# The second and the last unit of each feed-forward stage take the joined matmul form of the others

## The reference, cut to what matters

```
def _swiglu(h, w_gate, w_up, w_down):
    return (jax.nn.silu(h @ w_gate) * (h @ w_up)) @ w_down
x = x + 0.5 * _swiglu(_rmsnorm(x, g[0]), ffn_w_gate[layer, 0], ffn_w_up[layer, 0], ffn_w_down[layer, 0])
```

## Time and profile before

| What | Value |
|---|---|
| median of 3 runs | 1509.05 us (1508.98 to 1510.08) |
| the profiled execution's own time | 1512.8 us |
| its span | 1511.0 us |
| TensorE busy | 1488.1 us, 98% |
| TensorE weight loads | 1300.1 us, 86% |
| VectorE / ScalarE / GpSimd busy | 1128.9 / 835.3 / 474.2 us |
| joined up steps (line 648, 16 matmuls each) | 1808 matmuls, so 113 units |

### The profile page before, as it was taken

The page is one execution under the profiler, slowest core; times in us unless marked ns, Lnnn a source line. Parts: engine busy times, 40 slices in busy tenths (PEclk is TensorE's granted clock), DMA queues, the critical chain, the costliest instruction groups (busy, mean ns, idle before and its releaser), DMA issues. The chain is left out here.

```text
span 1511.0 us, 26410 instructions
## 1 busy us (share of the span) xinstructions
PE 1488.1 (98%) x9944; PEld 1300.1 (86%) x9944; DVE 1128.9 (75%) x1286; ACT 835.3 (55%) x1288; POOL 474.2 (31%) x209
## 2 busy tenths in 40 slices
PE   8999999999999999999999999999999999999998
PEld 7888889898888888888987888888888887888887
DVE  6877856567777777787765687877777789878785
ACT  6555465336545555545576645456455578654544
POOL 2443400000434327343352343433343300144342
PEclk9999999999999999999999999999999999999999
DMA  7655542134655546555442555555555553265552
GB/s 269 232 182 193 180 140 72 59 114 152 223 194 182 193 135 225 193 194 185 166 169 85 195 186 195 191 178 185 194 182 192 181 181 126 98 212 190 188 197 75
DMA packets 48815, 260.04 MB, mean 172 GB/s; under 512 B 5584, under 2 KB 5968, under 8 KB 28144
## 3 DMA queue, kind: packets, MB, share of 16 engines
q1 hardware_dynamic: 29520, 190.49, 36.1%
q10 hardware_dynamic: 19152, 68.53, 14.1%
q0 software_dynamic: 80, 0.14, 0.0%
HBM read 258.08 MB, written 1.05 MB: 171 GB/s over the span
## 5 line engine op out<-in xcount | busy, mean ns | idle before, releaser
L378 POOL TENSOR_TENSOR dn_lo<-raw_dn,dn_hi 128x1024 fp32r<-128x1024 f32 x138 | 435.8, 3158 | 791.1 <-ACT dn_hi L361 783.8
L365 DVE TENSOR_TENSOR gu_lo<-raw_gu,gu_hi 128x2048 fp32r<-128x2048 f32 x161 | 370.2, 2299 | 163.6 <-ACT gu_hi L351 162.0
L648 PE MATMUL banks<-h_both,gu_hi 128*128 128x512 f32 x1808 | 428.2, 389 | 0.0
L648 PEld LDWEIGHTS banks<-h_both,gu_hi 128*128 128x128 f32 x1808 | 339.3, 188 | 70.5
L559 DVE TENSOR_TENSOR act_lo<-act,act_hi 128x256 fp32r<-128x256 f32 x132 | 312.0, 2364 | 9.0 <-ACT act_hi L525 9.0
L351 ACT CAST gu_hi<-raw_gu 128x2048 fp32r<-128x2048 f32 x160 | 303.9, 1900 | 12.0 <-PE banks L385 12.0
L517 ACT COPY arena<-banks 128x256 f32<-128x256 f32 x113 | 42.1, 372 | 373.3 <-PE banks L656 373.3
L656 PEld LDWEIGHTS banks<-h_both,gu_lo 128*128 128x128 f32 x1808 | 231.8, 191 | 8.8
L656 PE MATMUL banks<-h_both,gu_lo 128*128 128x256 f32 x1808 | 234.5, 283 | 0.0
L385 PE MATMUL banks<-dn_hi,act_hi 128*128 128x512 f32 x528 | 207.9, 394 | 1.8 <-DVE act_lo L559 1.4
L385 PE MATMUL banks<-dn_lo,act_hi 128*128 128x512 f32 x528 | 207.1, 392 | 0.0
(11 more groups left out here) (390 smaller groups left out, 1648.6 us busy)
## 6 DMA issues: line engine op xcount, KB each, us to landing
raw_gu<-units_gu SPq DMA_DIRECT2D x161, 1024.0 KB, 4.8
raw_dn<-units_dn ACTq DMA_DIRECT2D x130, 512.0 KB, 3.5
raw_dn<-units_dn SPq DMA_DIRECT2D x32, 512.0 KB, 3.5
x<-x_in SPq DMA_DIRECT2D x2, 512.0 KB, 5.1
cst<-constants SPq DMA_DIRECT2D x1, 688.0 KB, 5.8
raw_gu<-units_gu SPq DMA_DIRECT2D x2, 256.0 KB, 6.2
raw_gu<-units_gu SPq DMA_DIRECT2D x1, 512.0 KB, 7.4
lora<-low_rank SPq DMA_DIRECT2D x1, 512.0 KB, 6.7
```

What stands on the lines that cost most here:

```text
L365: nc.vector.tensor_tensor(gu_lo[:, p, :], raw_gu[:, p, :], gu_hi[:, p, :].bitcast(F32), ALU.subtract).then_inc(gu_lo_ready, 1)
L378: nc.gpsimd.tensor_tensor(dn_lo[:, p, 0:n], raw_dn[:, p, 0:n], dn_hi[:, p, 0:n].bitcast(F32), ALU.subtract).then_inc(dn_lo_ready, 1)
L648: ins = nc.tensor.matmul(banks[:, 2 * p + side, :], gu_hi[:, p, w], h_both[:, k, :, :].rearrange("p i t -> p (i t)"), start=first and k == ...
```

## The change

FIRST_BOTH goes from 2 to 1 and LAST_BOTH from 20 to 21. Unit 1 and unit 21 of each of the six stages take the joined form, and so does unit 20 of the final stage: 6 + 6 + 1 = 13 units. Unit 0 stays separate. The special code of unit 1 goes (`high_first`, `second_up_high_first`, the branch `both` of `ffn_up`); in the first stage TensorE waits for the gate half of `gu_hi` before the gate matmuls and for the whole before the up matmuls (`gate_only`). The weights for a unit two ahead are split only where there is one (`if ahead`).

```diff
-        FIRST_BOTH, LAST_BOTH = 2, FFN_UNITS - 2
+        FIRST_BOTH, LAST_BOTH = 1, FFN_UNITS - 1
...
-            if both is not None:
+            if ahead and both is not None:
                 hi_gu(act, pair + 1, p)
...
-                lo_gu(dve, pair + 1, p)
+                if ahead:
+                    lo_gu(dve, pair + 1, p)
...
-        def ffn_up(pe, pair, p, f, both=True):
-            if both:
-                ffn_up_joined(pe, pair, p, f)
-                return
-            pe.wait_ge(gu_lo_ready, 2 * pair + p + 1)
-            count(pe, act_ready, f - 1)
-            for side in range(2):
-                for k in range(KD):
-                    w = slice((side * KD + k) * P, (side * KD + k + 1) * P)
-                    ins = three_products(banks[:, 2 * p, side * T:(side + 1) * T],
...
-        def ffn_up_joined(pe, pair, p, f):
-            pe.wait_ge(gu_hi_ready, 2 * pair + p + 1)
+        def ffn_up(pe, pair, p, f, gate_only=False):
+            if not gate_only:
+                pe.wait_ge(gu_hi_ready, 2 * pair + p + 1)
             count(pe, act_ready, f - 1)
             high_weights(p, 0)
+            if gate_only:
+                pe.wait_ge(gu_hi_ready, 2 * pair + p + 1)
             high_weights(p, 1)
...
-            ffn_act(act, b, 1, f + 1, True)
+            ffn_act(act, b, 1, f + 1, True, n + 1)
...
-            ffn_act(act, b + i, 1, f + 2 * i + 1, False, load=s + 1 < len(stages))
+            ffn_act(act, b + i, 1, f + 2 * i + 1, False, n + 2 * i + 1, load=s + 1 < len(stages))
...
-            ffn_dve(dve, b, 1, f + 1, True, None, SECOND_BANK, FIRST_UP_BANKS[1] if high_first(s) else None)
+            ffn_dve(dve, b, 1, f + 1, True, n + 1)
...
-            ffn_dve(dve, b + i, 1, f + 2 * i + 1, False)
+            ffn_dve(dve, b + i, 1, f + 2 * i + 1, False, n + 2 * i + 1)
...
-            if high_first(s):
-                second_up_high_first(pe, s)
-            else:
-                ffn_up(pe, b, 1, f + 1, both=False)
+            if s == 0:
+                pe.wait_ge(second_gate, 1)
+            ffn_up(pe, b, 1, f + 1, gate_only=s == 0)
```

More of the change, by code:

```diff
@@ L527, in ffn_act @@
                 hi_gu(act, pair + 1, p)
-        FIRST_UP_BANKS = (5, 3)
-        SECOND_BANK = 2
+        FIRST_UP_BANK = 5
         def seam_bank(s):
@@ L568, in ffn_first_up @@
                 pe.wait_ge(gu_lo_ready, 2 * pair + 1)
-            gate, up = banks[:, bank, 0:T], banks[:, FIRST_UP_BANKS[0] if s == 0 else bank, T:2 * T]
+            gate, up = banks[:, bank, 0:T], banks[:, FIRST_UP_BANK if s == 0 else bank, T:2 * T]
             def gate_part(part, b):
@@ L605, in ffn_first_up, with high_weights @@
             ins.then_inc(gu_used, 1)
[L607 to L612, removed]
-            for side in range(2):
-                if s == 0:
-                    pe.wait_ge((second_gate, gu_hi_ready)[side], side + 1)
-                else:
-                    pe.wait_ge(gu_hi_ready, 2 * pair + 2)
-                for k in range(KD):
-                    w = slice((side * KD + k) * P, (side * KD + k + 1) * P)
[L620 to L629, removed]
-        def ffn_up(pe, pair, p, f, both=True):
-            if both:
-                ffn_up_joined(pe, pair, p, f)
-                return
-            pe.wait_ge(gu_lo_ready, 2 * pair + p + 1)
-            count(pe, act_ready, f - 1)
-            for side in range(2):
-                for k in range(KD):
-                    w = slice((side * KD + k) * P, (side * KD + k + 1) * P)
-                    ins = three_products(banks[:, 2 * p, side * T:(side + 1) * T],
[L641 to L645, removed]
+        def high_weights(p, side):
             for k in range(KD):
@@ L648, in high_weights, with low_weights @@
                 ins = nc.tensor.matmul(banks[:, 2 * p + side, :], gu_hi[:, p, w],
-                                       h_both[:, k, :, :].rearrange("p i t -> p (i t)"), start=first and k == 0,
-                                       stop=not first and k == KD - 1, skip_group_check=not first)
+                                       h_both[:, k, :, :].rearrange("p i t -> p (i t)"), start=k == 0, stop=False)
             return ins
-        def low_weights(p, side, first=False):
+        def low_weights(p, side):
             for k in range(KD):
                 w = slice((side * KD + k) * P, (side * KD + k + 1) * P)
-                ins = nc.tensor.matmul(banks[:, 2 * p + side, 0:T], gu_lo[:, p, w], h_hi[:, k, :], start=first and k == 0,
-                                       stop=not first and k == KD - 1, skip_group_check=first)
-            return ins
-        def ffn_up_joined(pe, pair, p, f):
-            pe.wait_ge(gu_hi_ready, 2 * pair + p + 1)
+                ins = nc.tensor.matmul(banks[:, 2 * p + side, 0:T], gu_lo[:, p, w], h_hi[:, k, :], start=False,
+                                       stop=k == KD - 1)
+            return ins
+        def ffn_up(pe, pair, p, f, gate_only=False):
+            if not gate_only:
+                pe.wait_ge(gu_hi_ready, 2 * pair + p + 1)
             count(pe, act_ready, f - 1)
             high_weights(p, 0)
+            if gate_only:
+                pe.wait_ge(gu_hi_ready, 2 * pair + p + 1)
             high_weights(p, 1)
@@ L776, in ffn_all_act @@
             i = HALF - 1
-            ffn_act(act, b + i, 0, f + 2 * i, s + 1 < len(stages), n + 2 * i if s + 1 < len(stages) else None)
-            ffn_act(act, b + i, 1, f + 2 * i + 1, False, load=s + 1 < len(stages))
+            ffn_act(act, b + i, 0, f + 2 * i, s + 1 < len(stages), n + 2 * i)
+            ffn_act(act, b + i, 1, f + 2 * i + 1, False, n + 2 * i + 1, load=s + 1 < len(stages))
         def ffn_all_dve(dve, s):
@@ L804, in ffn_all_dve @@
             n = both_before(f)
-            ffn_dve(dve, b, 0, f, True, None, seam_bank(s), FIRST_UP_BANKS[0] if s == 0 else None)
-            ffn_dve(dve, b, 1, f + 1, True, None, SECOND_BANK, FIRST_UP_BANKS[1] if high_first(s) else None)
+            ffn_dve(dve, b, 0, f, True, None, seam_bank(s), FIRST_UP_BANK if s == 0 else None)
+            ffn_dve(dve, b, 1, f + 1, True, n + 1)
             with dve.Fori(1, HALF - 1) as i:
@@ L810, in ffn_all_dve @@
             i = HALF - 1
-            ffn_dve(dve, b + i, 0, f + 2 * i, s + 1 < len(stages), n + 2 * i if s + 1 < len(stages) else None)
-            ffn_dve(dve, b + i, 1, f + 2 * i + 1, False)
+            ffn_dve(dve, b + i, 0, f + 2 * i, s + 1 < len(stages), n + 2 * i)
+            ffn_dve(dve, b + i, 1, f + 2 * i + 1, False, n + 2 * i + 1)
             add_to_x(dve, s)
@@ L846, in ffn_all_pe @@
             i = HALF - 2
-            ffn_up(pe, b + 1 + i, 0, f + 2 + 2 * i, both=s + 1 < len(stages))
+            ffn_up(pe, b + 1 + i, 0, f + 2 + 2 * i)
             ffn_down(pe, b + i, 1, f + 1 + 2 * i, False, False)
-            ffn_up(pe, b + 1 + i, 1, f + 3 + 2 * i, both=False)
+            ffn_up(pe, b + 1 + i, 1, f + 3 + 2 * i)
             ffn_down(pe, b + 1 + i, 0, f + 2 + 2 * i, False, False)
```

## The result

The changed kernel takes 1529.24 us (median of 4 runs, 1526.37 to 1533.64) against 1509.09 us before (1508.98 to 1510.08): a ratio of 1.0132, 95% interval 1.0119 to 1.0145. It is slower by 20 us; 1527 were forecast. Its profiled execution took 1530.55 us.

What follows compares the result with a forecast made beforehand. TensorE, busy 98% of the span, was taken as the bound. Waits at unit 1 of 15.45 us less 1.54 saved gave +13.9, 1523.0 us from the 1509.05 median; 4.2 for clock falls made 1527 us, range 1520 to 1534.

Steps and rivals of the forecast that it cites:

- The saving of 0.22 us a joined unit: TensorE's up step: 5.54 us joined against 5.76 separate, so 2.86 us over 13 units if nothing else moves.
- The formula of the Trainium skill: Up step: N/2.4 + 2.5 ns a matmul, so 16 fewer save only 0.04 us a unit; the prediction followed the trace instead.
- Units 21 and 20 hidden: Last units: act_lo 2.45 us behind the up step, 0.29 us ahead of down(21), so the full 1.54 us is saved.
- Unit 1, the chain of 9.63 to 9.66 us from the L365 ahead: At down(1): act_lo ends that late, so TensorE waits 3.9 us in stage one, 2.9 in two, 3.7 in five.
- The fifth stage: Unit 1 there: late dn_hi and POOL's dn_lo add 0.79 us; wait 3.7 us at down(1), stage cost 3.17 us.
- The 6.85 us: Second stage, unit 1: time from the end of L365 to down(1); a shorter chain would cause no wait.
- Nothing at down(2): Unit 2, no longer the first joined unit: no TensorE wait, down(2) coming 8.29 us behind down(1).
- The sum without the clock: Whole kernel: 15.45 us of stage shifts at unit 1 less 1.54 saved at the last units, +13.9 us.
- The clock: Behind the six waits at down(1): granted clock falls to half, taken as three falls of 1.4 us, 4.2 us.
- At most 1.7 us: Bound on the cost of each half-clock stretch behind a wait: half of its 3.41 us, 0 to 10.2 in all.
- The rival of a faster kernel: Unit 1's chain is hidden, no wait at down(1), today's waits at unit 2 go: 1506.2 us, chance 0.03.

Runs made afterwards that it cites:

- experiment 1: Kernel before with only the last units joined (unit 21 of each stage, unit 20 of the final one), unit 1 separate: 1505.33 us against 1508.89.
- Experiment 6: Changed kernel plus eight matmuls of 512 columns that change nothing, on TensorE ahead of up(2) in each stage: 1523.03 us, ratio 1.0093 to the kernel before.
- experiment 7: Kernel before with act_hi and act_lo made ahead of the next weights in joined units 2 to 20, units 1 and 21 separate: 1506.21 us against 1509.62.
- Experiment 4: Changed kernel with act_hi and act_lo made ahead of the next weights in all joined units: 1501.29 us, ratio 0.9948 to the kernel before.
- experiment 2: Kernel before with only unit 1 of each stage joined, the last units separate: 1530.24 us against 1508.89.
- experiment 3: Changed kernel with act_hi and act_lo made ahead of the next weights in unit 1 alone: 1524.36 us, ratio 1.0096 to the kernel before.
- experiment 5: Changed kernel with POOL's dn_lo of unit 2 waiting for act_lo of unit 1 in each stage: 1515.16 us, ratio 1.0039 to the kernel before.

## Why the prediction was right

- **The saving of 0.22 us a joined unit:** right. 5.54 us for the up step in experiment 1 as forecast. The formula of the Trainium skill (TensorE: Matmul & The Clock Gate, Back-to-back issue gap) that the prediction set against it is stated there for a matmul by itself, without its weight load. Here each matmul has one (9736 of each in the page's line above), so the formula could not have decided this.
- **Units 21 and 20 hidden:** right, 2.45 us against the 2.75 us available in experiment 1. In the changed kernel one of them, at the end of the fourth stage, came 0.2 us late: its `act_lo` ended 2.8 us behind the up step.
- **Unit 1, the chain of 9.63 to 9.66 us from the L365 ahead:** right in place and size: 9.59 us in the second stage. The waits came out at 3.82, 2.65 (three more of 2.66) and 3.17 us, where 3.9, 2.9 and 3.7 stood. The fifth stage was the one worked out least well: POOL's late `dn_lo` was there, but it ended 2.77 us behind the L365 ahead, where 3.05 was taken, and the chain was 10.1 us, not 10.4. The 6.85 us from that L365 to a TensorE that is ready for down(1) stands in no row: the earlier trace rows give 7.02 (386.23 to 393.25), and 6.99 was measured in the second stage, so the waits of 2.9 came out at 2.65.
- **Nothing at down(2):** right, down(2) follows in all stages without a wait of any size. The sum without the clock, 13.9 us, agrees with the table: 23.5 - 9.7 = 13.8. Four stages agree with their terms to 0.15 us. That the whole agrees so closely is in part luck: the first stage was 0.3 us dearer than its term (it has the wait of 0.5 us at down(0)), the fifth 0.4 us cheaper.
- **The clock:** the mechanism was right, its size was not. I took three falls of 1.4 us, 4.2 in all. The trace shows five, for 9.7 us, so this term was undersized by more than half. "At most 1.7 us" failed too: two stretches lasted 6.83 us, and the one of the fourth stage cost 2.9. Experiment 6 gives 6 us for most of it in the median of whole runs. The runs of the changed kernel scatter by 7.3 us, those of the kernel before, beside them, by 1.1 and in the later rounds by up to 3.7. The record ties this to the clock: the four runs of the changed kernel, 1526.37, 1527.92, 1530.55 and 1533.64 us, have a mean granted clock of 0.993, 0.992, 0.990 and 0.989. What decides in one execution whether a wait is followed by a fall stays open.
- **What I left out:** the part outside the feed-forward stages, -6.0 us in the traced executions and by the estimate above some -2 us in the medians. It stood against the undersized clock term, so the forecast of 1527 came nearer to 1529.24 than its terms were; that part of the hit is luck. The cause of the even mixer's gain is open in part. Of the seven kernels built for this and the two at hand, the only two with the wait of 1.3 us at line 385 are the kernel before and experiment 7, the two that still have TensorE's code unchanged; the DMA queue that their pages call `instruction` has 45 packets in these two and 43 or 44 in the others. That speaks for the place of the code, not for the joined form; it was not tried by itself.
- **The rival of a faster kernel** was priced at 1506.2 us. Experiment 4 has its condition, a chain that is hidden, and took 1501.29: the price left out what the waits of the kernel before at unit 2 cost, 3.4 us by experiment 7, and 1.7 us of waits on issue.

## What to carry to other kernels

A busy engine's saving (0.22 us a unit) is the small term; first ask when its next input comes, from the row that shows the same chain elsewhere in the same trace. Where two kinds of a step have a different order of the same operations on a helper engine, the turn from one order to the other is where the bound engine waits, and moving the turn moves the wait; make the order the same in all, with what is needed next first. Where the clock fell at a wait of some 2.7 us, the wait cost 1.5 to 2.9 us more.

## What the runs showed of the hardware

- At TensorE's waits of 2.65 to 3.82 us the granted clock fell to 0.50 in five of six cases, for 3.41 or 6.83 us; two matmuls of 512 columns there began 0.42 us apart (38.43 and 38.85 in the first stage), where it is 0.23 us at the full clock (1059.32 and 1059.55 in the fifth). The length of the wait alone did not decide it. It stayed at 1.00 at 3.17 us (fifth stage), at 3.04 (fourth stage of experiment 2) and at 2.41 (second stage of experiment 3), and fell at 2.40 (fourth and sixth stage of experiment 3) and at 2.01 in the first stage of experiment 6, not at 1.97 in its fourth, nor at 1.68 in experiment 5. One wait of the even mixer, 2.05 to 2.08 us for the same operation in all nine traces, was followed by half the clock in six of them (behind 197.68 in the kernel before) and not in experiments 3, 4 and 7.
- A DVE subtraction of 256 elements with both inputs in SBUF took 0.42 us, and 2.56 to 2.63 us when POOL had begun a subtraction just before it. The Trainium skill (SBUF — State Buffer, "SBUF: two separate sides") says that DVE, in an operation with two inputs in SBUF, and a GpSimd operation that reads SBUF share a pair of ports, and that whichever starts first holds it for its whole instruction. By that rule 2.1 us of the operation is waiting, not work; the trace agrees, since in experiment 5 the same operation is back at 0.42 us once POOL starts behind it.
